# Row transfers of a mixture-of-experts stage, issued in two parts with indices read in place

## The reference

```python
order = jnp.argsort(e_flat).astype(jnp.int32)
dest = pstarts[e_sorted] + jnp.arange(n_pairs, dtype=jnp.int32) - starts[e_sorted]
tok_buf = jnp.zeros((rows,), jnp.int32).at[dest].set(order // TOP_K)
w_buf = jnp.zeros((rows,), jnp.float32).at[dest].set(weights.reshape(n_pairs)[order])
xb = xn[tok_buf].reshape(n_blocks, MOE_BLOCK, D_MODEL)
def expert_block(args):
    xblk, e = args
    hid = jax.nn.silu(xblk @ w_gate[e]) * (xblk @ w_up[e])
    return hid @ w_down[e]
yb = lax.map(expert_block, (xb, blk_expert)).reshape(rows, D_MODEL)
return jnp.zeros_like(xn).at[tok_buf].add(yb * w_buf[:, None].astype(yb.dtype))
```

## Time and profile before

| | |
|---|---|
| median of 3 runs | 1460.65 us (1458.46 to 1460.8) |
| the profiled execution | 1458.78 us, span 1457.2 us |
| PE, DVE, ACT, POOL busy over the span | 88%, 75%, 49%, 19% |
| first gather of an expert's rows issued | 1098.72 us |
| last scatter issued | 1443.96 us |
| DMA read and written over the span | 180.92 MB and 39.72 MB |

### The profile page before, as it was taken

How to read it: one execution, slowest core, us unless ns; L and a number is a source line. 1 busy time by engine, 2 the same in 40 slices (tenths; PEclk the granted TensorE clock), 3 DMA queues, 4 the chain that set the end, 5 groups by cost and what they waited for, 6 DMA issues and landing times. The chain is left out here.

```text
span 1457.2 us, 25067 instructions
## 1 busy us (share of the span) xinstructions
PE 1288.0 (88%) x8761; PEld 770.6 (53%) x8761; DVE 1096.8 (75%) x1305; ACT 710.6 (49%) x1167; POOL 271.6 (19%) x276
## 2 busy tenths in 40 slices
PE   4899999959999999999999788889956999788875
PEld 2456666656666666666666445545533555344432
DVE  5678888775869999999994744536574999787772
ACT  4656565645323443334432633314113988676672
POOL 1281000000000000000000000000142666422322
PEclk9999999979799999999999999999977999999997
DMA  8500000022212222122220044446674989899962
GB/s 296 160 10 1 0 0 0 28 81 70 67 33 78 81 66 81 47 77 69 74 75 15 16 171 157 150 179 221 248 286 170 330 316 360 324 339 325 326 224 33
DMA packets 51047, 203.44 MB, mean 140 GB/s; under 512 B 14464, under 2 KB 15552, under 8 KB 38400
## 3 DMA queue, kind: packets, MB, share of 16 engines
q1 hardware_dynamic: 32032, 156.92, 29.2%
q0 software_dynamic: 16656, 36.84, 9.6%
q10 hardware_dynamic: 2304, 8.95, 1.6%
HBM read 180.92 MB, written 39.72 MB: 151 GB/s over the span
## 5 line engine op out<-in xcount | busy, mean ns | idle before, releaser
L1194 DVE SCALAR_TENSOR_TENSOR big<-c_region,c_taps,big 128x1024 f32 (+1 forms) x120 | 153.0, 1275 | 4.0 <-ACT caT L931 4.0
L72 PE MATMUL c_psb<-xnT,w_taken 128*128 128x364 f16 x456 | 146.1, 320 | 2.3 <-DVE f_w_l L1089 2.3
L73 PE MATMUL c_psb<-xnT,w_taken 128*128 128x364 f16 x456 | 146.0, 320 | 0.0
L74 PE MATMUL c_psb<-xnT,f_w_l 128*128 128x364 f16 x456 | 145.9, 320 | 0.0
L1194 DVE SCALAR_TENSOR_TENSOR caT<-c_region,c_taps,caT 128x1024 f32<-128x1024 f32 x112 | 142.8, 1275 | 0.0
L72 PE MATMUL o_psH<-e_gu,big 128*128 128x512 f16 x256 | 100.2, 391 | 1.5 <-issue 1.4
L74 PE MATMUL o_psH<-e_gu,big 128*128 128x512 f16 x256 | 99.7, 390 | 0.0
L73 PE MATMUL o_psH<-e_gu,big 128*128 128x512 f16 x256 | 99.6, 389 | 0.0
L72 PE MATMUL c_psa<-xnT,w_taken 128*128 128x364 f16 x312 | 99.1, 318 | 0.0
L74 PE MATMUL c_psa<-xnT,f_w_l 128*128 128x364 f16 x312 | 99.0, 317 | 0.0
L73 PE MATMUL c_psa<-xnT,w_taken 128*128 128x364 f16 x312 | 99.0, 317 | 0.0
(11 more groups left out here) (357 smaller groups left out, 3492.6 us busy)
## 6 DMA issues: line engine op xcount, KB each, us to landing
e_gu<-w_gu SPq DMA_DIRECT2D x34, 1024.0 KB, 24.9
w_taken<-w_feat SPq DMA_DIRECT2D x48, 512.0 KB, 4.0
e_d<-w_dn SPq DMA_DIRECT2D x17, 1024.0 KB
xnT<-w_gu SPq DMA_DIRECT2D x14, 1024.0 KB
big<-w_gu SPq DMA_DIRECT2D x14, 1024.0 KB, 33.2
m_gates<-gates POOLq DMA_DIRECT2D x8, 1092.0 KB, 5.8
xnT<-w_dn SPq DMA_DIRECT2D x7, 1024.0 KB
big<-w_dn SPq DMA_DIRECT2D x7, 1024.0 KB
```

Of the source, the lines that this page charges most:

```text
L72: pe.matmul(out, stat[0], mov[0], start=start, stop=False)
L73: pe.matmul(out, stat[0], mov[1], start=False, stop=False)
L74: return pe.matmul(out, stat[1], mov[0], start=False, stop=stop)
L1194: dve.scalar_tensor_tensor(y_j, glu[:, p, j:j + SEQ], tap, y_j, op0=ALU.mult, op1=ALU.add).then_inc(tap_done, 1)
```

## The change

A gather or scatter of a block that belongs to its own expert is issued as two indirect transfers, the first of slots 0 to 95 and the second of slots 96 to 127. The row numbers are read directly from `pairs` and, for the second transfer, from a new tile `e_pairs_up`, which SP fills with a second small load of the table (its 32 rows lie in partitions 0 to 31). The copies to `e_idx` and `e_idx_y` and the wait for them are gone there. This form is written out for gathers 0 to 27 and scatters 0 to 22. The loop, which may meet blocks whose number is only known at run time, starts at round 5 instead of 0, so with `few` = 6 it runs once: gathers 28 to 31, scatters 23 to 26, and after it scatters 27 to 31. In this part a transfer keeps its 128 rows and its copied index. Since every block now counts up its semaphore by 32, each is followed, once it has landed, by a second transfer of 32 rows whose row numbers are all T (`nobody`), so that it moves no row. The waits of PE and ACT on gathers and scatters are for 32 per block.

```diff
@@ feed-forward phase, SP @@
             sp.dma_start(pairs[:, 0:NE], A["pair_dram"].rearrange("(p n) a -> p n a", p=P)[:, 0:NE]).then_inc(pairs_ld, 16)
+            sp.dma_start(pairs_up[:], A["pair_dram"].rearrange("(p n) a -> p n a", p=P)[LOW:BLK, 0:NE]).then_inc(up_ld, 16)
@@ POOL @@
+            def own_tokens(b):
+                return ((slice(0, LOW), pairs.bitcast(U32)[0:LOW, b, 0:1]),
+                        (slice(LOW, BLK), pairs_up[:].bitcast(U32)[:, b, 0:1]))
+
+            def gather_own(b):
+                p, u = b % 2, b // 2
+                if b > 1:
+                    pool.wait_ge(xg_ld[p], 32 * u)
+                    pool.wait_ge(xT_done, b - 1)
+                for rows, tokens in own_tokens(b):
+                    pool.indirect_dma_start(out=xg[rows, p], out_offset=None, in_=A["hn_dram"],
+                                            in_offset=bass.IndirectOffsetOnAxis(ap=tokens, axis=0),
+                                            bounds_check=T - 1, oob_is_err=False).then_inc(xg_ld[p], 16)
+
+            def scatter_own(b):
+                p, u = b % 2, b // 2
+                if b > 1:
+                    pool.wait_ge(y_st[p], 32 * u)
+                pool.wait_ge(y_out, b + 1)
+                for rows, tokens in own_tokens(b):
+                    pool.indirect_dma_start(out=A["y_all"], out_offset=bass.IndirectOffsetOnAxis(ap=tokens, axis=0),
+                                            in_=y_o[rows, p], in_offset=None, compute_op=ALU.add,
+                                            bounds_check=T - 1, oob_is_err=False).then_inc(y_st[p], 16)
...
@@ POOL, gather() and scatter(), which stay in the loop and after it @@
+                pool.wait_ge(xg_ld[p], 32 * u + 16)
+                pool.sem_inc(gather_go, 1)
+                pool.indirect_dma_start(out=xg[LOW:BLK, p], out_offset=None, in_=A["hn_dram"],
+                                        in_offset=bass.IndirectOffsetOnAxis(ap=nobody[:, 0:1], axis=0),
+                                        bounds_check=T - 1, oob_is_err=False).then_inc(xg_ld[p], 16)
...
+                pool.wait_ge(y_st[p], 32 * u + 16)
+                pool.sem_inc(scatter_go, 1)
+                pool.indirect_dma_start(out=A["y_all"],
+                                        out_offset=bass.IndirectOffsetOnAxis(ap=nobody[:, 0:1], axis=0),
+                                        in_=y_o[LOW:BLK, p], in_offset=None, compute_op=ALU.add,
                                         bounds_check=T - 1, oob_is_err=False).then_inc(y_st[p], 16)
@@ POOL, the order @@
+            pool.wait_ge(up_ld, 16)
+            for b in range(6):
+                gather_own(b)
...
+            for b in range(8, NE - 4):
+                gather_own(b)
+                scatter_own(b - 5)
+            pool.iota(nobody[:], [[0, 1]], base=T, channel_multiplier=0).then_inc(nobody_done, 1)
...
-            with pool.Fori(0, few) as v:
+            with pool.Fori(NE // 4 - 3, few) as v:
                 for q in range(4):
                     gather(4 * v + 8 + q, q % 2, 2 * v + 4 + q // 2)
                     scatter(4 * v + 3 + q, (q + 1) % 2, 2 * v + (q + 3) // 2)
@@ ACT, result() @@
-                    act.wait_ge(y_st[p], 16 * u)
+                    act.wait_ge(y_st[p], 32 * u)
@@ PE, turn() @@
-                pe.wait_ge(xg_ld[p], 16 * u + 16)
+                pe.wait_ge(xg_ld[p], 32 * u + 32)
```

More of the change, by code:

```diff
@@ L55 @@
 BLK = 128
+LOW = 96
 NOV = 16
@@ L1645, in ffn_phase @@
         pairs = big_f[:, rest + 2 * D:rest + 2 * D + 2 * NBLK].rearrange("p (b a) -> p b a", a=2)
+        pairs_up = sb("e_pairs_up", [BLK - LOW, NE, 2], F32)
+        nobody = sb("e_nobody", [BLK - LOW, 1], U32)
         idx = sb("e_idx", [P, 2], U32)
@@ L1729, in ffn_phase @@
                                     "scat", "ctl"))
+        up_ld, nobody_done = sem("e_up_ld"), sem("e_nobody")
         pairs_ld, late_ld, xg_zero, all_out = sem("e_pairs_ld"), sem("e_late_ld"), sem("e_xg_zero"), sem("e_all_out")
@@ L1859, in scatter_pairs, with gather @@
                                                 in_=pair[0:rows, k, t, :], in_offset=None).then_inc(scat, 16)
-            def gather(b, p, u, first=False):
-                if not first:
-                    pool.wait_ge(xg_ld[p], 16 * u)
+            def own_tokens(b):
[19 more added lines that the diff above has]
+                                            bounds_check=T - 1, oob_is_err=False).then_inc(y_st[p], 16)
+            def gather(b, p, u):
+                pool.wait_ge(xg_ld[p], 32 * u)
                 pool.tensor_copy(idx[:, p:p + 1], token(b)).then_inc(idx_done, 1)
                 pool.wait_ge(idx_done, b + 1)
-                if not first:
-                    pool.wait_ge(xT_done, b - 1)
+                pool.wait_ge(xT_done, b - 1)
                 pool.sem_inc(gather_go, 1)
@@ L1872, in gather, with scatter @@
                                         bounds_check=T - 1, oob_is_err=False).then_inc(xg_ld[p], 16)
-            def scatter(b, p, u, first=False):
-                if not first:
-                    pool.wait_ge(y_st[p], 16 * u)
+                pool.wait_ge(xg_ld[p], 32 * u + 16)
[3 more added lines that the diff above has]
+                                        bounds_check=T - 1, oob_is_err=False).then_inc(xg_ld[p], 16)
+            def scatter(b, p, u):
+                pool.wait_ge(y_st[p], 32 * u)
                 pool.tensor_copy(idx_y[:, p:p + 1], token(b)).then_inc(idx_y_done, 1)
@@ L1899, in _ @@
             pool.wait_ge(pairs_ld, 16)
[L1900 to L1910, removed]
+            pool.wait_ge(up_ld, 16)
+            for b in range(6):
+                gather_own(b)
+            scatter_own(0)
+            gather_own(6)
+            scatter_own(1)
+            gather_own(7)
+            scatter_own(2)
+            for b in range(8, NE - 4):
+                gather_own(b)
+                scatter_own(b - 5)
+            pool.iota(nobody[:], [[0, 1]], base=T, channel_multiplier=0).then_inc(nobody_done, 1)
+            pool.sem_inc(idx_done, NE - 4)
+            pool.sem_inc(idx_y_done, NE - 9)
             few = rounds(pool)
+            pool.wait_ge(nobody_done, 1)
             pool.wait_ge(late_ld, 16 * NOV + 16)
-            with pool.Fori(0, few) as v:
+            with pool.Fori(NE // 4 - 3, few) as v:
                 for q in range(4):
@@ L1918, in _ @@
                 scatter(4 * few + 3 + q, (q + 1) % 2, 2 * few + (q + 3) // 2)
-            pool.wait_ge(y_st[0], 32 * few + 64)
+            pool.wait_ge(y_st[0], 64 * few + 128)
             pool.sem_inc(all_out, 1)
-            pool.wait_ge(y_st[1], 32 * few + 64)
+            pool.wait_ge(y_st[1], 64 * few + 128)
             pool.sem_inc(all_out, 1)
```

## The result

| | before | after |
|---|---|---|
| median | 1460.62 us (4 runs) | **1524.24 us** (4 runs, 1521.66 to 1525.32) |
| ratio | 1 | 1.0433 (95%: 1.0416 to 1.045) |
| profiled execution, time and span | 1458.78, 1457.2 | 1521.66, 1519.9 |
| gather 28 is issued at | 1359.78 | 1360.67 |
| from there to the end of the span | 97.4 | 159.2 |

What follows compares the result with a forecast made beforehand. Weight transfers were taken to bind the middle, PE the first stage. Gather 28 at 1339.8 (20 us earlier) plus a 125.9 us chain gives 1465.7; with 7.1 and 1.6 added, 1474 us, range 1460 to 1495.

Steps and rivals of the forecast that it cites:

- Slower, and where: Whole kernel: a gain before gather 28 and a larger loss after it, 20 us gained, 35.6 given back; chance 0.62.
- Split transfers, blocks 0 to 27, gain 20 us: Before gather 28: 96 slots six to an engine save four row passages, 0.94 us a block; gather 28 at 1339.8.
- The free tenth: Middle stage, 1245 to 1361 us: DMA engines at 0.90 while weights bind, so a tenth of their time is free.
- The bounds of 16 and 24.6: Limits in us on the 20 us gained before gather 28; at 24.6 PE's pace takes over.
- Rival A, cheap landings: From gather 28 on: all thirteen landings at their quiet value, chain 103 us, total 1451.5 us; chance 0.14.
- Rival B: Before gather 28: the split brings 0 instead of 20 us, or memory is the limit; total 1494 us; chance 0.12.
- Rival C, POOL's pace: First stage: POOL's round grows by 3 us to 10.2 and binds, gather 28 at 1362, total 1497 us; chance 0.12.
- The prediction's sign of being wrong: Gather 28 issued at 1360 us or later, or landings of 4 to 6 us beside weights.
- its rule for telling B from C: With gather 28 late: B if DMA still has a free tenth, C if POOL has no idle time in PE's stage.
- The landings: From gather 28 on: POOL waits for thirteen landings in a row, 92.8 us together, the first two gathers and scatters beside weights.
- The gaps between landings, 12 x 2.5: From gather 28 on: after a landing 2.5 us until the next transfer, wait's end, POOL going on and copy; 30 us.
- The end: After the last landing: another empty transfer, about 3.1 us, then 7.1 us to the end of the span.

## Why the prediction was wrong, point by point

- **Slower, and where**: right. The loss lies in the part that waits for landings, in a chain of `y_all` and `xnT` landings, one empty transfer after each.
- **Split transfers, blocks 0 to 27, gain 20 us**: the step that failed first. Gather 28 came at 1360.67 instead of 1339.8. The free tenth was filled, 0.98, but mostly by longer packets: from 1250 to 1350 us 1.6% more weight bytes moved, and the weight queue's share went from 69.8% to 76.3%. The step multiplied four passages fewer by a price and held the weight packet at 0.336 us. It became 0.362 because gathers were split. For the scatters' half of the step, 10 of the 20 us, the price was right: alone they gained 11. The gathers' half cost 17 instead of gaining 10. The bounds of 16 and 24.6 came from the passage price and from PE's pace, and had nothing for a side effect on the other queue.
- **Rival A, cheap landings**: did not come; beside weights the landings took 8.4 to 12.1 us.
- **Rival B**: its time before gather 28 was the one that came. Its reasons did not: memory was not the limit (384 GB/s), and with split scatters the balance did bring time. The Trainium skill (DMA: Bandwidth & Descriptors, Rules for kernel authors) advises against two transfers to disjoint partition halves. For these partly empty transfers the runs agree for gathers, by 17 us, and not for scatters, by 11.
- **Rival C, POOL's pace**: POOL was busy for 19.46 us more in some 14 rounds, its idle time before a gather shrank from 1.88 to 0.75 us, and the pace went from 9.02 to 9.16, where 10.2 was feared. Even this little is not shown to be POOL's, since the kernel with split gathers alone is slower there with POOL idle. The prediction's sign of being wrong, gather 28 at 1360 or later, came; its rule for telling B from C had no place for the true cause, a slower second queue.
- **The landings**: right, 94.7 against 92.8 us, with 8.86 and 8.42 us for the gathers beside weights (8.1 used) and 12.06 and 10.05 for the scatters beside weights (10.5 used). The last weight packets went at about 1411, where 1420 was used.
- **The gaps between landings, 12 x 2.5**: the second term that failed. From 1360.67 to the last empty transfer at 1506.67 lie 146.0 us; less 94.7 for landings and 0.9 from the last landing to that issue, 50.4 are left, 4.2 for each of twelve. The step priced the empty transfer by when POOL could go on after an ordinary one, 1.0 us. But a gather's empty transfer held POOL for 1.60 to 2.90 us, 0.9 instead of 0.2 passed between a landing and the empty issue, and a copy took up to 1.44 instead of 0.20. That is 20 us. Without the empty transfers the gaps average 1.9 us, so it is their price that was wrong.
- **The end**: 13.2 us from the last empty issue to the end of the span instead of 10.2.
- **The sum**: predicted 1474. The missing gain is 21, the gaps 20, the landings 2, the end 3, and the wait from the last landing to the last empty issue 1: 47, and 1474 + 47 = 1521, against the profiled 1521.66.
- **The range** ended at 1495, as the misses were taken one at a time: the missing gain with the chain as forecast, or POOL's pace with it. No case had both a lost gain and a longer chain.

## What to carry to other kernels

Before pieces of a transfer are handed to other DMA engines, ask what those engines and the places that they write are doing for the other queue: look at the time of that queue's packets, not at the share of busy engines, which rises in either case. Where an indirect transfer is partly empty, deal the used rows out over all partitions and leave the transfer whole; here that gained 25 us where splitting lost 7. And count a wait for a landing on the issuing engine by its whole round: the landing, the time until the engine goes on, every instruction that it then issues, an empty transfer too, and the next copy.

## What the runs showed of the hardware

A DMA share near 1.00 went with anything from 327 to 384 GB/s from 1250 to 1350 us: 0.98 and 327 in the change, 1.03 and 345 split at 64, 1.02 and 384 with interleaved slots. A weight packet of 8 KB took 0.358 to 0.370 us where gathers were issued in two parts and 0.315 to 0.336 where they were whole, split scatters or not. An indirect transfer in which no row is moved was not cheap: it held POOL for 0.9 to 2.9 us, and thirteen of them cost 29 to 30 us in a chain. One completion of an indirect transfer may count a semaphore up by 32, which replaces a transfer that serves only to count.
